# Two mixture-of-experts stages: what the gather of token rows reads, when the residual rows are formed, and the order around them

## The reference, cut to what matters

```python
x = layer_norm(DEEPNORM_ALPHA * x + mixed, ln1_g[layer], ln1_b[layer])
ffn = moe_ffn(x, router_w, router_b, exp_w_gate[layer], exp_w_up[layer], exp_w_down[layer])
x = layer_norm(DEEPNORM_ALPHA * x + ffn, ln2_g[layer], ln2_b[layer])

def layer_norm(x, g, b):
    mu, var = x.mean(-1), square(x - mu).mean(-1)
    return (x - mu) * rsqrt(var + LN_EPS) * g + b

def moe_ffn(x, ...):
    scores = sigmoid(x @ router_w)            # best group of four experts, best two in it
    # of every token's two experts e:  gate_e * ((silu(x @ w_gate[e]) * (x @ w_up[e])) @ w_down[e])
```

## Time and profile before

| | us |
|---|---|
| three timed runs | 1316.83, 1320.81, 1320.6 (median 1320.6) |
| profiled execution, time | 1317.5 |
| profiled execution, span | 1315.7 |
| PE busy | 1241.0 (94%) |
| DVE, ACT, POOL busy | 848.5 (64%), 619.4 (47%), 99.3 (8%) |
| mean granted clock of PE | 0.979 |
| read from HBM | 255.88 MB, 195 GB/s over the span |

### The profile page before, as it was taken

How to read it: one execution, slowest core, us unless ns; L and a number is a source line. 1 busy time by engine, 2 the same in 40 slices (tenths; PEclk the granted TensorE clock), 3 DMA queues, 4 the chain that set the end, 5 groups by cost and what they waited for, 6 DMA issues and landing times.

```text
span 1315.7 us, 17485 instructions
## 1 busy us (share of the span) xinstructions
PE 1241.0 (94%) x7044; PEld 668.6 (51%) x7048; DVE 848.5 (64%) x1060; ACT 619.4 (47%) x689; POOL 99.3 (8%) x60
## 2 busy tenths in 40 slices
PE   8999999999999999999999987999979989799996
PEld 4676565456654444656657643433435555343333
DVE  6687675988774487555568676333766677843366
ACT  5466556345553364444447523233634583332361
POOL 1000000000000014000014140000003102100000
PEclk9999999999999999999999987999989999799998
DMA  9475434665755665656650017599945600569990
GB/s 319 143 258 162 136 127 160 232 207 165 228 200 192 198 244 180 210 193 204 211 183 11 2 65 255 179 347 364 382 135 186 222 9 32 183 209 339 359 379 36
DMA packets 152812, 258.09 MB, mean 196 GB/s; under 512 B 8913, under 2 KB 81692, under 8 KB 152732
## 3 DMA queue, kind: packets, MB, share of 16 engines
q1 hardware_dynamic: 152732, 256.98, 58.1%
HBM read 255.88 MB, written 1.07 MB: 195 GB/s over the span
## 4 chain that ended last, share of the span: by engine, by line
PE 78%; DVE 9%; ACT 5%; DMA 4%; issue 2%; DVEq 1%; SPq 1%; POOL 1%; ACTq 0%; POOLq 0%
PE ps L1107 12%; PE ps L820 9%; PE ps L801 8%; PE ps L1374 7%; PE ps L1151 6%; PE ps L1109 6%; PE ps L1419 4%; DVE w_ring L2069 3%; DMA w_ring<-in_exp_w_down 3%; PE ps L1067 3%; PE ps L1357 3%; PE ps L838 3%; PE ps L1294 2%; PE ps L1478 2%; PE ps L1441 1%
## 5 line engine op out<-in xcount | busy, mean ns | idle before, releaser
L2069 DVE SCALAR_TENSOR_TENSOR w_ring<-w_ring,w_hi 128x2048 f16<-128x2048 f32 (+3 forms) x164 | 366.5, 2242 | 140.4 <-ACT w_hi L1627 139.6
L1627 ACT ACTIVATE w_hi<-w_ring 128x2048 f16<-128x2048 f32 (+3 forms) x164 | 303.2, 1855 | 207.0 <-PE ps L1151 50.9
L1107 PE MATMUL ps<-actT,w_hi 128*128 128x512 f16 x608 | 197.8, 379 | 0.0
L1109 PE MATMUL ps<-actT,w_ring 128*128 128x256 f16 x608 | 165.7, 273 | 0.0
L1627 ACT ACTIVATE arena<-ps 128x256 f16<-128x256 f32 (+8 forms) x121 | 79.6, 675 | 154.5 <-PE ps L1109 69.8
L820 PE MATMUL ps<-w_hi,actT 128*128 128x512 f16 x384 | 116.7, 379 | 2.9 <-DVE w_ring L2069 2.9
L801 PE MATMUL ps<-w_hi,actT 128*128 128x512 f16 (+2 forms) x384 | 112.9, 371 | 2.5 <-DVE actT L2074 2.5
L1107 PEld LDWEIGHTS ps<-actT,w_hi 128*128 128x128 f16 x608 | 59.5, 98 | 71.7
L1374 PE MATMUL ps<-arena 128*128 128x512 f16 x240 | 74.1, 415 | 10.5 <-DVE arena L2069 8.1
L694 POOL TENSOR_TENSOR stats<-stats 128x1 f32<-128x1 f32 x14 | 16.5, 1181 | 800.2 <-DVE stats L2741 506.3
L1961 ACT ACTIVATE arena<-ps 128x256 f32<-128x256 f32 x32 | 12.2, 382 | 134.2 <-PE ps L1374 88.2
(11 more groups left out here) (453 smaller groups left out, 2135.2 us busy)
## 6 DMA issues: line engine op xcount, KB each, us to landing
w_ring<-in_dil_w_in SPq DMA_DIRECT2D x36, 1024.0 KB, 5.2
w_ring<-in_w_ff SPq DMA_DIRECT2D x32, 1024.0 KB, 5.2
w_ring<-in_exp_w_down SPq DMA_DIRECT2D x26, 1024.0 KB, 10.2
w_ring<-in_w_in SPq DMA_DIRECT2D x24, 1024.0 KB, 5.1
w_ring<-in_exp_w_gate SPq DMA_DIRECT2D x48, 512.0 KB, 7.9
w_ring<-in_exp_w_up SPq DMA_DIRECT2D x48, 512.0 KB, 8.7
w_ring<-in_sb_w_in SPq DMA_DIRECT2D x12, 1024.0 KB, 5.4
w_ring<-in_w_branch SPq DMA_DIRECT2D x8, 1024.0 KB, 4.9
```

The costliest lines, as they stand in the source:

```text
L1107: pe.matmul(ps[:, bank + c, :], w_h[:, k, cols], aT[:, kk, :], start=(kk == 0), stop=False, skip_group_check=True)
L1109: ins = pe.matmul(ps[:, bank + c, 0:S], w_l[:, k, cols], aT[:, kk, 0:S], start=False, stop=(kk == KD - 1), skip_group_check=True)
L1627: return act.activation(dst, src, ACT.Copy, scale=scale)
L2069: dve.scalar_tensor_tensor(out=lo16(h)[:, 0:kn * c], in0=slot(h)[:, 0:kn * c], scalar=W_POW, in1=hi16(h)[:, 0:kn * c], op0=ALU.mult, op1=A ...
```

## The change

- x_hi and x_lo are made of x_norm (no scale by 8, no wait for x_full) and lie in actT's place; x_norm stays whole. x_hi stands between silu(0) and silu(1).
- The scale and bias are put on behind the gather: in fills 0 to 7 inside the same instruction; in fills 8 to 15 ACT first writes float32 rows (`x_rows`, two buffers in y's place), drains, and then makes the high part; DVE makes the low part from x_rows.
- GpSimd's `full` in the experts waits for moe_h 9 of its layer.
- The turn of tile 1 stands before router(0). One of the two splits behind fills 0 and 1 moves ahead of them, on DVE ahead of the last one_hots. Gathers and gates are dealt to the units anew.
- actT is a ninth slot once unit 7's up is done. Outside the experts 6 high buffers are used rather than 4.
- SBI0's first two splits move to before silu(15) (on DVE weigh(15)) and behind its turn.
- The semaphores of the head turns of the first block are merged in pairs.

The diff without those semaphores and a few lines that follow from the rest:

```diff
-SPLIT_EARLY = {2: 1, 3: 1, 7: 1, 12: 1, 14: 1}
-SPLIT_LATE = {2: 1, 4: 1, 7: 1, 9: 3, 11: 3, 12: 1, 13: 3, 14: 1}
+SPLIT_EARLY = {2: 1, 3: 1, 7: 2, 12: 1, 14: 1}
+SPLIT_LATE = {2: 1, 4: 1, 9: 3, 11: 3, 12: 1, 13: 3, 14: 1}
-FILLS_UP = {3: (4,), 4: (6,), 5: (16,), 6: (10,), 7: (13,), 10: (18,)}
-FILLS_TURN = {2: (2,), 3: (5,), 4: (7,), 5: (8,), 6: (11,), 7: (14,)}
-FILLS_DOWN = {2: (3,), 5: (9,), 6: (12,), 7: (15, 17)}
+FILLS_UP = {2: (2,), 3: (4,), 4: (6,), 5: (8,), 6: (12,), 10: (18,)}
+FILLS_TURN = {2: (3,), 3: (5,), 4: (7,), 5: (9,), 6: (13,)}
+FILLS_DOWN = {4: (16,), 5: (10, 11), 6: (14, 15), 7: (17,)}
...
+    if _key == EXPERT_HALVES[0]:
+        _slot[RING + 2] = _h + RELEASES.index(up_halves(7)[-1]) + 1
...
-        _s = min(range(RING + 2 if _late else RING), key=lambda s: (_slot[s], s))
-        _b = min(range(8 if _late else 6 if _key else 4), key=lambda b: (_hi[b], b))
+        _s = min(range(RING + (0 if not _late else 2 if _key == RELEASES[-1] else 3)), key=lambda s: (_slot[s], s))
+        _b = min(range(8 if _late else 6), key=lambda b: (_hi[b], b))
...
-        SLOT_MORE = (arena[:, 9216:11264], arena[:, 20480:22528])
+        SLOT_MORE = (arena[:, 9216:11264], arena[:, 20480:22528], actw)
...
-        x_hi, x_lo = (half(xnw[:, o:o + D]).rearrange("p (t n) -> p t n", t=T) for o in (0, D))
+        x_hi, x_lo = (half(actw[:, o:o + D]).rearrange("p (t n) -> p t n", t=T) for o in (0, D))
...
@@ GpSimd @@
-                    if m == 1:
-                        pool.wait_ge(sig("qkv_out"), 22)
+                    pool.wait_ge(sig(("moe_h", "qkv_out", "moe_h")[m]), (9, 22, NU + 9)[m])
                     full((6, 7, 8)[m], True)
...
@@ PE @@
                 up(0)
+                turn_tile(turn, 1)
                 pe.wait_ge(sig("ld_router"), 16)
                 router(0)
-                turn_tile(turn, 1)
...
@@ ACT @@
+        def gains_of(layer):
+            def gain(f):
+                c = NPROW + 32 * layer + f % 8
+                return pcol[:, c:c + 1], pcol[:, c + 8:c + 9]
+            return gain
...
                         if f < 8:
-                            ins = copy(xg_f[:, f, :], src)
+                            ins = copy(xg_f[:, f, :], src, *gain(f))
                         elif f < 16:
-                            ins = copy(xg_hi[:, f - 8, :], src)
+                            copy(x_rows[:, f % 2, :], src, *gain(f))
+                            act.drain()
+                            ins = copy(xg_hi[:, f - 8, :], x_rows[:, f % 2, :], A_POW)
...
                 silu(0)
+                copy(x_hi, x_norm[:, :, :]).then_inc(sig("route_act"), 1)
                 silu(1)
                 h_high(0)
                 h_high(1)
-                act.wait_ge(sig("x_full"), 2 * layer + 2)
-                copy(x_hi, x_tok[:, :, :], A_POW).then_inc(sig("route_act"), 1)
+                splits(1)
                 fills((0, 1))
-                splits(2)
+                splits(1)
                 for i in range(2, NU):
                     splits(SPLIT_EARLY.get(i, 0))
+                    if i == NU - 1 and layer == 0:
+                        hi(2 * SBI0)
                     silu(i)
...
                     splits(SPLIT_LATE.get(i, 0))
+                    if i == NU - 1 and layer == 0:
+                        hi(2 * SBI0 + 1)
...
                 h_high(NU - 1)
-                if layer == 0:
-                    hi(2 * SBI0)
-                    hi(2 * SBI0 + 1)
...
@@ DVE @@
                         if f < 8:
-                            ins = dve.tensor_copy(xg_f[:, f, :], src)
+                            ins = scaled(xg_f[:, f, :], src, *gain(f))
                         elif f < 16:
                             dve.wait_ge(sig("route_act"), ACT_STEPS * layer + FILL_ACT[f])
-                            ins = dve.tensor_tensor(xg_lo[:, f - 8, :], src, xg_hi[:, f - 8, :], ALU.subtract)
+                            ins = dve.scalar_tensor_tensor(out=xg_lo[:, f - 8, :], in0=x_rows[:, f % 2, :], scalar=A_POW,
+                                                           in1=xg_hi[:, f - 8, :], op0=ALU.mult, op1=ALU.subtract)
...
-                dve.scalar_tensor_tensor(out=x_lo, in0=x_tok[:, :, :], scalar=A_POW, in1=x_hi, op0=ALU.mult, op1=ALU.subtract)\
-                    .then_inc(sig("route_dve"), 1)
+                dve.tensor_tensor(x_lo, x_norm[:, :, :], x_hi, ALU.subtract).then_inc(sig("route_dve"), 1)
                 rank_gates()
+                splits(1)
                 one_hots(0, 128, 0, 4)
                 few_gates()
                 fills((0, 1))
-                splits(2)
+                splits(1)
```

More of the change, by code:

```diff
@@ L186 @@
 SLOT, SLOT_FREE, LANDED, HI_BUF, HI_FREE, SPLIT_NO = [], [], [], [], [], []
-_slot, _landed, _hi = [0] * (RING + 2), [0] * (RING + 2), [0] * 8
+_slot, _landed, _hi = [0] * (RING + 3), [0] * (RING + 3), [0] * 8
 for _h in range(NH):
@@ L456, in build @@
         at[0] = 4096
-        y_hi, y_lo = (half(take(D // 2)) for _ in range(2))
+        u_y = take(D)
+        y_hi, y_lo = (half(u_y[:, o:o + D // 2]) for o in (0, D // 2))
+        x_rows = u_y.rearrange("p (b s) -> p b s", b=2)
         hT_hi, hT_lo = (half(take(DE)).rearrange("p (b n) -> p b n", b=2) for _ in range(2))
@@ L939, in _ @@
             pe.wait_ge(sig("kv_out"), 1)
-            head_turns(q_tok, "qT_pe")
+            head_turns(q_tok, "heads_pe")
             evacuated(g)
@@ L944, in _ @@
             pe.wait_ge(sig("k_roped"), 1)
-            pe.wait_ge(sig("qT"), 1)
-            head_turns(k_tok, "kT_pe")
+            pe.wait_ge(sig("heads"), 1)
+            head_turns(k_tok, "heads_pe")
             def mla_score(h):
                 if h == 0:
-                    pe.wait_ge(sig("kT"), 1)
+                    pe.wait_ge(sig("heads"), 2)
                 else:
@@ L1716, in _ @@
                            scale=1.0 / SUM_POW).then_inc(sig("out_by_act"), 1)
-            act.wait_ge(sig("qT_pe"), 1)
-            copy(qT[0:QKD, :, :], ps[0:QKD, 4:8, :].rearrange("p b (h s) -> p (b h) s", h=2)).then_inc(sig("qT"), 1)
+            act.wait_ge(sig("heads_pe"), 1)
+            copy(qT[0:QKD, :, :], ps[0:QKD, 4:8, :].rearrange("p b (h s) -> p (b h) s", h=2)).then_inc(sig("heads"), 1)
             hi(21)
@@ L1728, in _ @@
             act.activation(sp_e[:, :], sp_e[:, :], ACT.Ln, bias=1.0).then_inc(sig("sp_ln"), 1)
-            act.wait_ge(sig("kT_pe"), 1)
-            copy(kT[0:QKD, :, :], ps[0:QKD, 4:8, :].rearrange("p b (h s) -> p (b h) s", h=2)).then_inc(sig("kT"), 1)
+            act.wait_ge(sig("heads_pe"), 2)
+            copy(kT[0:QKD, :, :], ps[0:QKD, 4:8, :].rearrange("p b (h s) -> p (b h) s", h=2)).then_inc(sig("heads"), 1)
             hi(23)
@@ L1934, in experts @@
                 nth = [3]
+                gain = gains_of(layer)
                 def splits(n):
@@ L1961, in silu @@
                     act.activation(e_silu[:, i % 2, :], ps[:, 4 + i % 2, 0:DE], ACT.Silu,
-                                   scale=1.0 / (A_POW if is_pair(i) else SUM_POW)).then_inc(sig("moe_silu"), 1)
+                                   scale=1.0 if is_pair(i) else 1.0 / SUM_POW).then_inc(sig("moe_silu"), 1)
                 def h_high(i):
@@ L2934, in fills @@
                         if f < 8:
-                            ins = dve.tensor_copy(xg_f[:, f, :], src)
+                            ins = scaled(xg_f[:, f, :], src, *gain(f))
                         elif f < 16:
                             dve.wait_ge(sig("route_act"), ACT_STEPS * layer + FILL_ACT[f])
-                            ins = dve.tensor_tensor(xg_lo[:, f - 8, :], src, xg_hi[:, f - 8, :], ALU.subtract)
+                            ins = dve.scalar_tensor_tensor(out=xg_lo[:, f - 8, :], in0=x_rows[:, f % 2, :], scalar=A_POW,
+                                                           in1=xg_hi[:, f - 8, :], op0=ALU.mult, op1=ALU.subtract)
                         elif f == FILL_GATES:
                             dve.tensor_scalar(r_few[:, 0:4], ps[:, 6, 0:40:13], A_POW / SUM_POW, None, ALU.mult)
-                            dve.tensor_copy(r_few[0:64, 4:8], ps[0:64, 6, 52:95:14])
-                            ins = dve.tensor_copy(r_few[64:P, 4:8], ps[64:P, 6, 53:96:14])
+                            dve.tensor_scalar(r_few[0:64, 4:8], ps[0:64, 6, 52:95:14], A_POW, None, ALU.mult)
+                            ins = dve.tensor_scalar(r_few[64:P, 4:8], ps[64:P, 6, 53:96:14], A_POW, None, ALU.mult)
                         else:
@@ L2961, in experts @@
                 fills((0, 1))
-                splits(2)
+                splits(1)
                 for i in range(2, NU):
                     splits(SPLIT_EARLY.get(i, 0))
+                    if i == NU - 1 and layer == 0:
+                        lo(2 * SBI0)
                     if i == 6:
@@ L2972, in experts @@
                     splits(SPLIT_LATE.get(i, 0))
+                    if i == NU - 1 and layer == 0:
+                        lo(2 * SBI0 + 1)
```

(3 more changed lines are left out.)

## The result

The changed kernel took 1301.3 us (median of four runs, 1298.7 to 1301.9) against 1319.6 for the kernel before (1316.8 to 1320.8): ratio 0.9858, 95% interval 0.9840 to 0.9876, about 18.3 us off. The forecast was 1300, 18.4 off. Its profiled execution has a span of 1300.1 us, 15.6 shorter. Of the 2.7 us that this lacks to 18.3, 1.8 arise before layer 0's experts: up(0) ends at 775.77 and at 777.54 now. The only edit that works there, the merged semaphores, does not explain it: all changed kernels have it, and their profiles fall on two levels (775.4 to 776.0, or 777.1 to 777.5).

A forecast was written before the change was run, and what follows sets the result against it. PE, busy 94% of the span, was taken as the bound, with saturated transfers binding the expert stages too. Terms 7.7 + 5.4 + 4.4 + 1.9 - 1.0 = 18.4 us off 1317.5 gave 1299.1, stated as 1300, range 1288 to 1311.

The forecast's parts named there:

- The start: Start of each expert stage, up(0)'s end to up(2)'s: 9 us shorter in layer 0, 7.5 in layer 1.
- The end: End of layer 0's expert stage: the add no longer waits for two splits, the turn comes 4.4 us earlier.
- The entry of the attention: Entry of the stick-breaking attention: six high buffers free the last splits, so the first sb_clip comes earlier; 1.9 us gained.
- The middle: Each layer's up(2)'s end to down(14)'s end: 1.8 us longer in layer 0, 2.6 in layer 1.
- Later releases of slots: Units 6 and 7: gathers moved earlier delay slot releases, and so the transfers, against PE; 2.6 us lost a layer.
- The copies and the drain: ACT's extra copies and drain in fills 8 to 15: hidden, no cost; if not, up to 5 us a layer.
- Ninth slot: Expert stage's transfers: one goes ahead of its release and closes a gap; 1.3 us gained in layer 0, 0.5 in layer 1.
- GpSimd's rows: Middle of each expert stage, from weigh(8) on: four operations beside DVE's splits cost 0.5 us a layer, bounds 0 and 5.5.
- A: Rival: the saturated transfers absorb the gains at the starts, only end and entry remain; 1311 us, chance 0.12.
- B: Rival: PE alone decides, so the starts gain 9+2 and 7.5+2 us; 1291 us, chance 0.10.
- C: Rival: GpSimd holds DVE in the middle, some eight splits and y_lows a layer, 2.8 us each; 1343 us, chance 0.04.
- D: Rival: nothing measurable, extra copies and GpSimd's rows eat the rest of the gain; 1319 us, chance 0.04.

The follow-up runs named there:

- e1: Changed kernel with GpSimd's residual rows in the experts run as early as before, beside the start of the stage; 1309.8 us, ratio 0.9928.
- e2: Changed kernel with router(0) ahead of the turn of tile 1, as before; 1304.5 us, ratio 0.9874.
- e3: Changed kernel with both splits of the first gathered expert behind fills 0 and 1, as before; 1307.2 us, ratio 0.9906.
- e4: Changed kernel with the next projection's two splits at the end of layer 0's stage, ahead of the residual add, as before; 1305.0 us, ratio 0.9897.
- e8: Changed kernel with 4 high buffers outside the experts rather than 6; 1299.3 us, ratio 0.9838.
- e6: Changed kernel without the ninth slot and with gathers, gates and splits dealt to the units as before; 1305.1 us, ratio 0.9874.
- e11: Changed kernel with old dealing, no ninth slot, and fills 8 to 15 straight from PSUM, their scale and bias left out; 1300.7 us, ratio 0.9855.
- e10: Changed kernel with gathers 14 and 15 behind up(7) and the ninth slot one unit later; 1297.5 us, ratio 0.9823.
- e5: Changed kernel without the ninth slot; 1301.0 us, ratio 0.9848.
- e7: Changed kernel with GpSimd's residual rows one unit later, behind weigh(9) instead of weigh(8); 1303.4 us, ratio 0.9884.
- e9: Changed kernel with 20 idle matmuls instead of 8 ahead of the projection; 1301.2 us, ratio 0.9853.
- e12: Changed kernel with gathers 14 and 15 behind up(7), ninth slot one unit later, and 20 idle matmuls ahead of the projection; 1294.9 us, ratio 0.9812.

## Why the prediction was right, and where it was not

**The sum (18.4; measured 18.3).** That the two agree to 0.1 us is luck. The stretches gained 17.4 us: 3.9 less than forecast at the starts, the end and the entry, and 2.9 more in the middles.

**The start (9 and 7.5; measured 8.5 and 6.9).** Right in cause and size. GpSimd's rows beside DVE are its largest part (e1: 4.2 and 4.7, the prediction took 5), then the turn before the router (e2: 3.0 and 2.0, of which it named 1.7), then the split ahead of the fills (e3: 1.9 each). Whether up(1) would win back its full clock was left open (5.2 or 7.1 us); it took 6.93, near the slow end.

**The end (4.4; measured 4.2, e4 4.2).** Right. What it set off behind the turn, 0.8 us in e4, the prediction did not look at.

**The entry of the attention (1.9; measured 0, e8).** The step that failed. Its first half came about: the first exp is 2.1 us earlier against the projection's end. Its second, "ACT limited again by the s=5 copy", is short of a step: that copy waits for PE, which gives 1.2 us of the 1.9, and 13 us later ACT waits 0.91 for DVE's sb_clip (1051.79), which used to hide behind ACT. A chain followed only to its next wait was priced as if it ran to the end. "Between" even grew by 0.7: with the turn 4.2 us earlier the idle matmuls run at full clock and end early, so that the projection starts 0.9 us sooner behind the turn. But PE stands 2.83 us ahead of it, after which 24 matmuls took 7.0 us and not 5.3. That they need not is shown by e2, e6 and e11.

**The middle (+1.8 and +2.6; measured +0.4 and +1.1).** Near, but by terms that cancel:
- Later releases of slots, -2.6 a layer: the cost exists (the wait before up(10) and the clock behind it, 4.4 us together; e10 takes 1.5 of it back), but the dealing as a whole saves 2.4 and 2.6 where the sum made it cost 2.6 (e6 against e5), since it removes a wait that had become 3.5 us with the lower clock behind it. This term failed too, by 5 us a layer.
- The copies and the drain, priced at nothing as hidden: in the old dealing they cost 2.9 and 3.6 us (e11). In the new one no run leaves them out; with copies and new dealing together the middles are 0.9 and 1.1 us longer than before (e5). That the forecast of the middles came within 1.5 us, with terms wrong by 3 to 5 us, is luck. The prediction priced each edit against the kernel before; these two had to be priced together.
- Ninth slot, 1.3 and 0.5: measured 0.6 and 0.0 (e5).
- GpSimd's rows, 0.5 a layer: nearly nothing, because they run in 872.8 to 882.3, before DVE's splits. One unit later the middles are 0.7 and 2.2 longer (e7), and a split beside the rows grows by up to 2.1, not by the 1.1 of the earlier trace rows.

**The rivals.** A falls by e1 to e3, whose later starts left the middles alone. B asked for middles 2 us shorter and they are longer, by 0.4 and 1.1. C's hold of a whole GpSimd operation is about right in size, its count is not: two a layer, not eight, and none in the changed kernel. D falls by the result.

## What to carry to other kernels

Price an edit that adds latency together with the edit that moves the place where this latency is waited for; alone, each of the two here had the wrong sign or size. When a stretch full of transfers starts later and keeps its length (e1 to e3), nothing in it hangs on a fixed time, so a gain ahead of it is kept in full. Before a difference of one spell of lower clock (1.7 us here) is put down to an edit, see whether kernels without the edit show it as well. Where an engine is held by a neighbour, move the neighbour's work into a time in which the engine rests, and look at the place again when the order around it changes.

## What the runs showed of the hardware

- A break of PE costs more than its length, but not always. Behind 2.05 us (e11) the granted clock stayed 1.00, behind 3.49 (e6) it was 0.68 for 5.3 us. At one and the same place it went either way: behind 2.09 us in the attention 0.70 (e9) and 1.00 (e12), a difference of 1.6 us, and behind 2.83 us ahead of the projection 0.68 (changed kernel) and 1.00 (e6), 1.7 us. So the length of a break alone does not tell. Behind 5.90 us (e4) eight small matmuls took 1.97 us instead of 1.09.
- A GpSimd row operation takes 2.34 us with DVE nearly at rest, and 4.3 us beside DVE's splits (8.58 for two in e7), while a split went from 2.29 to 4.43. Both engines lose, since they take turns by whole instructions.
- A copy from PSUM whose scale and bias come from columns is dearer for ACT: a fill took 0.78 us, before 0.60. The prediction allowed 0.1. ACT's timeline of the kernel before, then of the changed one:

```profile
805.09 0.60 ACT L1627 ACTIVATE arena<-ps 128x512 f32<-128x512 f32 x1 [9.51 <-PE ps L1478]
```

```profile
802.41 0.78 ACT L1635 ACTIVATE arena<-ps,pcol 128x512 f32<-128x512 f32 x1 [0.80 <-PE ps L1479]
```
